# The value product of latent attention in two passes over paired high and low weights, with a later hand-over of each pair's result

## The chip, the cores and the metric

One core of a Trainium2 chip runs the whole kernel. The metric is the device time of one execution in microseconds (us); smaller is better. The matrix engine is PE (its weight loads are listed as PEld), the vector engine DVE, the scalar engine ACT, GpSimd POOL, and SP issues the transfers. Each engine executes its own list of instructions in order and waits on semaphores for the others.

## The reference, cut to what matters

Two layers of a decoder trunk over 512 tokens of width 1024: a layer with latent attention, a layer with an mLSTM mixer, each followed by a squared-ReLU MLP. The change is inside the attention of the first layer: 16 heads, query and key width 96, value width 64, in blocks of 128 queries that see the keys up to their own block.

```
for blk in range(S // ATTN_BLOCK):                       # 4 blocks of 128 queries
    s = (q_n . k_n + q_r . k_r) * scale                  # 128 x k_end per head
    p = softmax(where(k_idx <= q_idx, s, -inf))
    outs.append(einsum('bhqk,bhkd->bqhd', p, v[:, :k_end]))
o = concatenate(outs, axis=1).reshape(B, S, 16 * 64)
return o @ w_o
```

## The kernel before

Every float32 factor x is split into x_hi, a copy rounded to the matrix engine's fp32r format, and x_lo = x - x_hi, also in fp32r. A product of two such factors is three matmuls: hi by lo, hi by hi, lo by hi. ACT mostly makes the high parts (a cast), DVE or POOL the low ones (a subtraction).

Attention runs over 16 heads in 8 pairs. Every engine has a function `attention(head)`, and the order of its calls is written out by hand; it is that order that decides who waits behind whom. A head passes through these steps:

- `q_half(head + 2, ...)` on PE: the query product of the head after next, 12 matmuls of 512 columns in two halves. `q_table` (DVE) scales it into `qtmp`, `q_high` (ACT) and `q_low` (DVE) split it. In odd heads `k_high` (ACT, two casts of 64x512) and `k_low` (DVE, two subtractions of 64x512) split the keys of the next pair, which `k_product` (PE, even heads) made.
- `turn_p(head, b)` on PE for b = 0..3: transposes the (b + 1) probability blocks of query block b into PSUM. `pt_high` (ACT) and `pt_low` (DVE) split them into `pth` and `ptl`. `turn_p(head, b)` may not start before `pt_low` has emptied the bank two steps back (`t_lo`).
- `scores(head + 1, b)` on PE: the scores of the next head, in a ring of three PSUM banks. `row_max` (DVE) and `exp` (ACT) empty them. `scores(head + 1, 3)` reuses the bank of b = 0, so it waits for `exp(head + 1, 0)` (semaphore `s_exp`).
- `weigh(head)` on PE: the value product. A 128x128 weight tile holds the values of 128 keys. The tensors `vh` and `vl` have three column groups of 64: the pair's even head, zeros, the odd head. The window of 128 columns that starts at 64 * e covers the head's values and the zeros, so both heads of a pair accumulate into one PSUM bank, `B_PV`, rows 0 to 63 and 64 to 127. It makes three passes of four matmuls (512, 384, 256 and 128 columns): `vh` by `pth`, `vl` by `pth`, `vh` by `ptl`.
- After the second head of a pair, `turn_scales` and `spread_scales` (PE), `row_scales` (DVE), `rows_turned` and `rows_spread` (ACT) bring the reciprocal row sums into `r_b`. At the start of the next even head `o_scaled` (DVE) multiplies bank `B_PV` by `r_b` into `o_norm(i)`, `o_high` (ACT) rounds it into `uh` and `o_low` (POOL) makes `ul`. `weigh` of the next even head waits for `o_scaled` (semaphore `o_new`).
- `strip_low` on POOL makes the low parts of the weight strip that a head three steps ahead needs (`split` on ACT makes the high ones).

`attention_end` replaces the last two heads on PE: with no further queries to make, it puts parts of the output projection (`out_products(k)`, six matmuls of 512 columns each, which need `uh` and `ul` of pair k, semaphore `o_lo`) between the steps, and `out_products(5..7)` after the last `weigh`.

Of the kernel before, what the change touches and what calls it, by code (L numbers as in the profile page):

```python
# [5 lines left out]
F32 = mybir.dt.float32  # L6
F32R = mybir.dt.float32r
I32 = mybir.dt.int32
ALU = mybir.AluOpType
# [5 lines left out]
P = 128  # L15
# [87 lines left out]
def trunk(nc, a, out):  # L103
    ctx = ExitStack()
    with ctx:
# [5 lines left out]
        def sem(name):  # L111
            return ctx.enter_context(nc.semaphore(name))
# [69 lines left out]
        cql = A("cql", [P, 4, S], F32R)  # L182
        ckvh = A("ckvh", [P, 2, S], F32R)
        ckvl = A("ckvl", [P, 2, S], F32R)
        vh = A("vh", [P, TT, 3 * VD], F32R)
        vl = A("vl", [P, TT, 3 * VD], F32R)
        prob = A("prob", [P, P * TT * (TT + 1) // 2])
        cos = A("cos", [P, S])
        sin = A("sin", [P, S])
# [24 lines left out]
        def v_slot(i):  # L214

            return v_all[:, i, :].rearrange("p (t e n) -> p t e n", t=TT, e=2)

        def heads_of(t):

            return t[:, :, :].rearrange("p t (r n) -> p t r n", r=3)[:, :, 0::2, :]  # L220

        def gap_of(t):

            return t[:, :, VD:2 * VD]

        def prob_of(b):

# [3 lines left out]
        def o_norm(i):  # L231

            return diag[:, i % 2, :]
# [57 lines left out]
        def bank(b):  # L291
            return ps[:, b, :]
# [49 lines left out]
        v_hi, v_lo = sem("v_hi"), sem("v_lo")  # L342
        s_mm, s_max, s_exp = sem("s_mm"), sem("s_max"), sem("s_exp")
        t_mm, t_hi, t_lo = sem("t_mm"), sem("t_hi"), sem("t_lo")
        w_mm, o_new, o_hi, o_lo = sem("w_mm"), sem("o_new"), sem("o_hi"), sem("o_lo")
        r_inv, rt_mm, rt_ready, r_mm, r_ready, pick_ready = (sem("r_inv"), sem("rt_mm"), sem("rt_ready"), sem("r_mm"),
                                                             sem("r_ready"), sem("pick_ready"))
# [224 lines left out]
        def _(pool):  # L572
# [15 lines left out]
            g.tensor_copy(onesr[:], ones[:, 0:2])  # L588
            g.tensor_copy(identr[:], ident[:])
            g.tensor_copy(maskr[:], mask_s[:]).then_inc(consts, 1)  # L590
            for t in (vh, vl):
                g.memset(gap_of(t).bitcast(F32), 0.0)

            def norm_adds(norm, end=False):

# [12 lines left out]
            def strip_low(n, kind, p=0):  # L608

                pool.wait_ge(whi_ready, p * 2 + (n + 1))  # L610
                for src, hi, lo in split_parts(kind, n % 2):
                    last = g.tensor_tensor(lo, src, hi.bitcast(F32), ALU.subtract)
                last.then_inc(wlo_ready, 1)
# [17 lines left out]
            def v_low(i):  # L631

                pool.wait_ge(v_hi, i + 1)
                g.tensor_tensor(heads_of(vl), v_slot(i), heads_of(vh).bitcast(F32), ALU.subtract).then_inc(v_lo, 1)

            def o_low(i):

                pool.wait_ge(o_hi, i + 1)
                g.tensor_tensor(ul[:, i, :], o_norm(i), uh[:, i, :].bitcast(F32), ALU.subtract).then_inc(o_lo, 1)
# [4 lines left out]
            for head in range(HEADS):  # L644
                if head % 2 == 0:
                    v_low(head // 2)
                    if head:
                        o_low(head // 2 - 1)
                if head + 3 < HEADS:
                    strip_low(N_PAIR + head + 3, "kq" if head % 2 else "q")  # L650
                elif head + 3 < HEADS + 2:
                    strip_low(N_WO + head + 3 - HEADS, "full")

            def low_hidden(layer, q, lead, per):
                for j in range(8):
# [76 lines left out]
        def _(act):  # L732
# [116 lines left out]
            def exp(head, b):  # L849

                z = 4 * head + b
                act.wait_ge(s_max, z + 1)
                if head:
                    act.wait_ge(t_mm, z - 3)
                sc.activation(prob_of(b), ps[:, B_S + z % S_RING, 0:P * (b + 1)], ACT.Exp,
                              bias=nmax[:, b:b + 1],
                              accum_out=rsum[:, 4 * (head % 2) + b:4 * (head % 2) + b + 1]).then_inc(s_exp, 1)

            def pt_high(head, b):

                z = 4 * head + b
                if b == 0 and head >= 2:
                    act.wait_ge(w_mm, head - 1)
                act.wait_ge(t_mm, z + 1)
                sc.copy(pth[head % 2][:, 0:b + 1, P * b:P * b + P],
                        ps[:, B_PT + z % 2, 0:P * (b + 1)].rearrange("p (j q) -> p j q", q=P)).then_inc(t_hi, 1)

            def v_high(i):

                if i:  # L870
                    act.wait_ge(w_mm, 2 * i)
                sc.copy(heads_of(vh), v_slot(i)).then_inc(v_hi, 1)

            def o_high(i):

                act.wait_ge(o_new, i + 1)
                sc.copy(uh[:, i, :], o_norm(i)).then_inc(o_hi, 1)
# [37 lines left out]
            def attention(head):  # L915

                i, second = head // 2, head % 2
                nxt = head + 1 < HEADS
                if not second:
                    v_high(i)  # L920
                    if i:
                        o_high(i - 1)
                elif nxt:
                    for e in range(2):
                        k_high(e, i + 1)
                pt_high(head, 0)
                pt_high(head, 1)
                if head + 3 < HEADS:
                    split(N_PAIR + head + 3, "q" if not second else "kq")
                elif head + 3 == HEADS:  # L930
                    split(N_WO)
                if second:
                    rows_turned(i)
                pt_high(head, 2)
                if nxt:
                    exp(head + 1, 0)
                pt_high(head, 3)
                if nxt:
                    exp(head + 1, 1)
                if head + 2 < HEADS:  # L940
                    q_high(head + 2)
                if nxt:
                    exp(head + 1, 2)
                    exp(head + 1, 3)
                if second:
                    rows_spread(i)
                if head + 2 == HEADS:
                    split(N_WO + 1)

            for head in range(HEADS):  # L950
                attention(head)
            o_high(PAIRS - 1)

            def residual_stage(n0, t0, norm, gain):
# [188 lines left out]
        def _(dve):  # L1143
# [176 lines left out]
            def row_scales(i):  # L1320
# [5 lines left out]
                own.link(v.tensor_copy(rinv2[:, 0:8], rinv[:]))  # L1326
                low(rinv2[:, 8:16], rinv[:], rinv2[:, 0:8]).then_inc(r_inv, 1)

            def o_scaled(i):

                dve.wait_ge(w_mm, 2 * i + 2)
                dve.wait_ge(r_ready, i + 1)
                if i >= 2:
                    dve.wait_ge(o_lo, i - 1)
                v.tensor_tensor(o_norm(i), bank(B_PV), r_b[:], ALU.mult).then_inc(o_new, 1)

            for e in range(2):
                k_low(e, 0)
# [6 lines left out]
            def attention(head):  # L1345

                nxt = head + 1 < HEADS
                i, second = head // 2, head % 2
                if second:
                    row_scales(i)  # L1350
                elif i:
                    o_scaled(i - 1)
                if second and nxt:
                    for e in range(2):
                        k_low(e, i + 1)
                pt_low(head, 0)
                pt_low(head, 1)
                if head + 2 < HEADS:
                    q_table(head + 2)
                if nxt:  # L1360
                    row_max(head + 1, 0)
                pt_low(head, 2)
                if nxt:
                    row_max(head + 1, 1)
                    row_max(head + 1, 2)
                pt_low(head, 3)
                if nxt:
                    row_max(head + 1, 3)
                if head + 2 < HEADS:
                    q_low(head + 2)  # L1370

            for head in range(HEADS):
                attention(head)
            o_scaled(PAIRS - 1)
            dve.wait_ge(o_lo, PAIRS - 1)
            dve.wait_ge(o_hi, PAIRS)
# [244 lines left out]
        def _(pe):  # L1621
# [177 lines left out]
            def weigh(head):  # L1799

                e = head % 2
                cols = slice(VD * e, VD * e + P)
                pe.wait_ge(t_hi, 4 * head + 4)
                pe.wait_ge(v_hi, head // 2 + 1)
                if e == 0 and head:
                    pe.wait_ge(o_new, head // 2)
                for j in range(TT):
                    mm(ps[:, B_PV, P * j:S], vh[:, j, cols], pth[e][:, j, P * j:S], start=(e + j == 0), stop=False)
                pe.wait_ge(v_lo, head // 2 + 1)
                for j in range(TT):  # L1810
                    mm(ps[:, B_PV, P * j:S], vl[:, j, cols], pth[e][:, j, P * j:S], start=False, stop=False)
                pe.wait_ge(t_lo, 4 * head + 4)
                for j in range(TT):
                    last = mm(ps[:, B_PV, P * j:S], vh[:, j, cols], ptl[e][:, j, P * j:S], start=False,
                              stop=(e == 1 and j == TT - 1))
                last.then_inc(w_mm, 1)

            def turn_scales(i):
# [376 lines left out]
```

## Time and profile before

| | |
|---|---|
| Median of 3 runs | 1213.28 us (1212.80 to 1213.59) |
| The profiled execution's own time | 1213.74 us |
| Span of its trace | 1211.8 us |
| PE busy | 1201.4 us, 99% of the span |
| DVE, ACT, POOL busy | 602.2, 455.1, 278.9 us |
| Attention, from about 79 us to 225 us of the span | PE, DVE, ACT and POOL all work |

How to read the trace's rows: the time at which a row starts, its duration, the engine, the source line, what is written and read, and how many instructions are merged in the row. A square bracket gives the time that the engine sat idle before the row and what ended it. Starts of matmuls overlap the ends of the ones before: the distance between two starts is what a matmul costs PE, and the duration shown is its latency. A busy PE may therefore still hide waits shorter than that latency.

### The profile page before, as it was taken

What the parts mean: (1) busy time and instruction counts of PE and PEld (TensorE: products, weight loads), DVE (VectorE), ACT (ScalarE), POOL (GpSimd) and SP (SyncE); (2) the same over time, 40 slices, a digit from 0 to 9 for tenths busy, and PEclk for the clock granted to TensorE, in tenths of its full rate; (3) what the DMA queues carried; (4) which work ended last, traced back from release to release, by engine and by line L of the source; (5) the groups of instructions that cost most, each with busy time, mean ns of one, the idle gap of its engine ahead of it and who ended that gap; (6) DMA issues with size and microseconds to landing.
All of it is one profiled execution on the core that took longest, in us unless ns stands there. A gap on an engine that the chain in (4) does not pass through costs nothing.

```text
span 1211.8 us, 15769 instructions
## 1 busy us (share of the span) xinstructions
PE 1201.4 (99%) x6130; PEld 1016.2 (84%) x6130; DVE 602.2 (50%) x818; ACT 455.1 (38%) x734; POOL 278.9 (23%) x286
## 2 busy tenths in 40 slices
PE   9999999999999999999999999999999999999998
PEld 8878888888888888888879899988888888888887
DVE  6766666455334334344357645657443443433432
ACT  5567777433212222123344255644321221222234
POOL 2324234242002002012212145633210110210212
PEclk9999999999999999999999999999999999999999
DMA  6111113232333323322233534513233233332221
GB/s 202 40 35 29 34 26 105 71 104 70 105 104 102 99 78 104 104 93 81 77 100 104 148 92 98 114 38 99 75 105 104 74 102 103 104 104 82 93 74 70
DMA packets 117513, 107.42 MB, mean 89 GB/s; under 512 B 21350, under 2 KB 115780, under 8 KB 117452
## 3 DMA queue, kind: packets, MB, share of 16 engines
q1 hardware_dynamic: 117420, 106.56, 29.2%
q8 instruction: 43, 0.70, 0.3%
q14 instruction: 18, 0.15, 0.0%
q10 hardware_dynamic: 32, 0.01, 0.0%
HBM read 104.45 MB, written 2.11 MB: 88 GB/s over the span
## 4 chain that ended last, share of the span: by engine, by line
PE 82%; DVE 1%; issue 0%; ACT 0%; POOLq 0%; POOL 0%; DVEq 0%; ACTq 0%
PE ps L1630 25%; PE ps L1632 25%; PE ps L1631 25%; PE ps L2072 1%; PE ps L2074 1%; PE ps L2073 1%; PE ps L2101 1%; PE ps L2103 0%; PE ps L2102 0%; PE ps L1924 0%; PE ps L1926 0%; PE ps L1925 0%; PE ps L2084 0%; PE ps L1994 0%; PE ps L1656 0%
## 5 line engine op out<-in xcount | busy, mean ns | idle before, releaser
L747 ACT CAST whi<-raw 128x2048 fp32r<-128x2048 f32 (+4 forms) x148 | 183.0, 1266 | 262.1 <-PE ps L1632 254.7
L1151 DVE TENSOR_TENSOR wlo<-raw,whi 128x2048 fp32r<-128x2048 f32 (+3 forms) x90 | 197.6, 2198 | 151.9 <-ACT whi L747 151.8
L1630 PE MATMUL ps<-xl,whi 128*128 128x512 f32 (+1 forms) x624 | 245.1, 393 | 0.1
L1631 PE MATMUL ps<-xh,whi 128*128 128x512 f32 (+1 forms) x624 | 242.9, 389 | 0.0
L1632 PE MATMUL ps<-xh,wlo 128*128 128x512 f32 (+1 forms) x624 | 242.9, 389 | 0.0
L1630 PE MATMUL ps<-ul,whi 128*128 128x512 f32 x576 | 224.7, 390 | 0.3 <-DVE wlo L1151 0.3
L1632 PE MATMUL ps<-uh,wlo 128*128 128x512 f32 x576 | 224.2, 389 | 0.0
L1631 PE MATMUL ps<-uh,whi 128*128 128x512 f32 x576 | 224.1, 389 | 0.0
L657 POOL TENSOR_TENSOR ul<-sq,uh 128x512 fp32r<-128x512 f32 x64 | 83.7, 1308 | 521.1 <-ACT uh L1000 521.1
L1382 DVE TENSOR_TENSOR h<-ps,h 128x512 f32<-128x512 f32 x78 | 53.6, 689 | 181.5 <-PE ps L1632 178.0
L1000 ACT CAST uh<-sq 128x512 fp32r<-128x512 f32 x64 | 39.7, 620 | 266.3 <-DVE sq L1414 266.3
L1630 PEld LDWEIGHTS ps<-xl,whi 128*128 128x128 f32 (+1 forms) x624 | 116.6, 187 | 26.4 <-issue 1.9
L1631 PEld LDWEIGHTS ps<-xh,whi 128*128 128x128 f32 (+1 forms) x624 | 116.6, 187 | 25.5 <-issue 1.0
L1632 PEld LDWEIGHTS ps<-xh,wlo 128*128 128x128 f32 (+1 forms) x624 | 116.6, 187 | 25.1
L1630 PEld LDWEIGHTS ps<-ul,whi 128*128 128x128 f32 x576 | 108.1, 188 | 22.9 <-DVE wlo L1151 0.7
L1632 PEld LDWEIGHTS ps<-uh,wlo 128*128 128x128 f32 x576 | 108.1, 188 | 22.6
L1631 PEld LDWEIGHTS ps<-uh,whi 128*128 128x128 f32 x576 | 108.1, 188 | 22.3
L1408 DVE TENSOR_TENSOR diag<-ps,r_a 128x512 f32<-128x512 f32 x64 | 44.0, 688 | 105.6 <-PE ps L1632 105.6
L602 POOL TENSOR_TENSOR acc<-acc,sq 128x512 f32<-128x512 f32 x30 | 48.7, 1623 | 128.2 <-ACT sq L761 127.6
L1630 PE MATMUL ps<-wlo,xh 128*128 128x256 f32 x256 | 73.5, 287 | 0.0
L1631 PE MATMUL ps<-whi,xh 128*128 128x256 f32 x256 | 72.4, 283 | 0.0
L1632 PE MATMUL ps<-whi,xl 128*128 128x256 f32 x256 | 72.4, 283 | 0.0
(276 smaller groups left out, 1689.3 us busy)
## 6 DMA issues: line engine op xcount, KB each, us to landing
raw<-in_mlp_w SPq DMA_DIRECT2D x64, 1024.0 KB, 5.2
raw<-in_mlstm_w_in SPq DMA_DIRECT2D x12, 1024.0 KB, 5.3
raw<-in_mla_w_o SPq DMA_DIRECT2D x4, 1024.0 KB, 4.9
raw<-in_mlstm_w_o SPq DMA_DIRECT2D x4, 1024.0 KB, 5.2
raw<-in_mla_w_uq SPq DMA_DIRECT2D x16, 192.0 KB, 2.5
x_tok<-in_x SPq DMA_DIRECT2D x4, 512.0 KB, 6.9
raw<-in_mla_w_in SPq DMA_DIRECT2D x2, 1024.0 KB, 5.7
mx<-m_rows SPq DMA_DIRECT2D x8, 256.0 KB, 3.8
```

The lines of the kernel that those rows point to most:

```text
L602: g.tensor_tensor(acc[:], acc[:], sq[:, k % 2, :], ALU.add).then_inc(acc_add, 1)
L657: g.tensor_tensor(ul[:, j, :], sq[:, j % 2, :], uh[:, j, :].bitcast(F32), ALU.subtract) \
L747: last = sc.copy(hi, src)
L1000: sc.copy(uh[:, m, :], sq[:, m % 2, :]).then_inc(u_hi, 1)
L1151: last = v.tensor_tensor(lo, src, hi.bitcast(F32), ALU.subtract)
L1382: return v.tensor_tensor(h[:, m, :], bank(t % RING), h[:, m, :], ALU.add)
L1408: v.tensor_tensor(diag[:, m % 2, :], bank((t0 + m) % RING), r_a[:], ALU.mult) \
L1630: mm(o, ah, bl, start=first, stop=False)
L1631: mm(o, ah, bh, start=False, stop=False)
L1632: ins = mm(o, al, bh, start=False, stop=last)
L2072: mm(o[:, 0:VW], hi, mvh[:, e, j, :], start=(j == 0), stop=False)
L2073: mm(o[:, 0:P], hi, mvl[:, e, j, :], start=False, stop=False)
```

## The change

The columns of high and low values stand side by side in one tensor `vhl` of four groups of 64: even head high, even head low, odd head low, odd head high. `weigh` uses the 128 columns of the head as weights, so one pass over `pth` gives both the high and the low value product, in the two halves of the bank's rows; a second pass over `ptl` completes it. Each head now fills the whole bank, so it is emptied head by head: `o_second` (ACT) moves the half that belongs to the low columns into `o_part` in SBUF, at the rows of the other half, and `o_add` (DVE) adds the two into `o_norm(i)`. `weigh(head)` waits for `o_add` of the head before (`o_sum`). `o_scaled` now multiplies `o_norm(i)` by `r_b` in SBUF, and stands, as do `o_high` and `o_low`, at the end of the next even head and no longer at its start; on POOL `strip_low` comes ahead of `o_low`.

```diff
-        vh = A("vh", [P, TT, 3 * VD], F32R)
-        vl = A("vl", [P, TT, 3 * VD], F32R)
+        vhl = A("vhl", [P, TT, 4 * VD], F32R)
+        o_part = A("o_part", [P, S])
...
+        def v_parts(low):
+
+            quarters = vhl[:, :, :].rearrange("p t (r n) -> p t r n", r=4)
+            return quarters[:, :, 1:3, :] if low else quarters[:, :, 0::3, :]
...
-            for t in (vh, vl):
-                g.memset(gap_of(t).bitcast(F32), 0.0)
...
                 if head % 2 == 0:
                     v_low(head // 2)
-                    if head:
-                        o_low(head // 2 - 1)
                 if head + 3 < HEADS:
                     strip_low(N_PAIR + head + 3, "kq" if head % 2 else "q")
                 elif head + 3 < HEADS + 2:
                     strip_low(N_WO + head + 3 - HEADS, "full")
+                if head % 2 == 0 and head:
+                    o_low(head // 2 - 1)
...
+            def o_second(head):
+
+                e = head % 2
+                act.wait_ge(w_mm, head + 1)
+                if head >= 2:
+                    act.wait_ge(o_sum, head - 1)
+                sc.copy(o_part[64 * e:64 * e + 64, :], ps[64 - 64 * e:128 - 64 * e, B_PV, :]).then_inc(o_moved, 1)
...
                     v_high(i)
-                    if i:
-                        o_high(i - 1)
...
                 pt_high(head, 1)
+                if head:
+                    o_second(head - 1)
...
                     exp(head + 1, 3)
+                if i and not second:
+                    o_high(i - 1)
...
+            o_second(HEADS - 1)
             o_high(PAIRS - 1)
...
+            def o_add(head):
+
+                i, rows = head // 2, slice(64 * (head % 2), 64 * (head % 2) + 64)
+                dve.wait_ge(o_moved, head + 1)
+                if head % 2 == 0 and i >= 2:
+                    dve.wait_ge(o_lo, i - 1)
+                v.tensor_tensor(o_norm(i)[rows, :], ps[rows, B_PV, :], o_part[rows, :], ALU.add).then_inc(o_sum, 1)
+
             def o_scaled(i):
 
-                dve.wait_ge(w_mm, 2 * i + 2)
+                dve.wait_ge(o_sum, 2 * i + 2)
                 dve.wait_ge(r_ready, i + 1)
-                if i >= 2:
-                    dve.wait_ge(o_lo, i - 1)
-                v.tensor_tensor(o_norm(i), bank(B_PV), r_b[:], ALU.mult).then_inc(o_new, 1)
+                v.tensor_tensor(o_norm(i), o_norm(i), r_b[:], ALU.mult).then_inc(o_new, 1)
...
                 if second:
                     row_scales(i)
-                elif i:
-                    o_scaled(i - 1)
...
                     q_table(head + 2)
+                if head:
+                    o_add(head - 1)
                 if nxt:
                     row_max(head + 1, 0)
...
                     q_low(head + 2)
+                if i and not second:
+                    o_scaled(i - 1)
...
+            o_add(HEADS - 1)
             o_scaled(PAIRS - 1)
...
-                cols = slice(VD * e, VD * e + P)
+                cols = slice(P * e, P * e + P)
                 pe.wait_ge(t_hi, 4 * head + 4)
-                pe.wait_ge(v_hi, head // 2 + 1)
-                if e == 0 and head:
-                    pe.wait_ge(o_new, head // 2)
+                pe.wait_ge(v_lo, head // 2 + 1)
+                if head:
+                    pe.wait_ge(o_sum, head)
                 for j in range(TT):
-                    mm(ps[:, B_PV, P * j:S], vh[:, j, cols], pth[e][:, j, P * j:S], start=(e + j == 0), stop=False)
-                pe.wait_ge(v_lo, head // 2 + 1)
-                for j in range(TT):
-                    mm(ps[:, B_PV, P * j:S], vl[:, j, cols], pth[e][:, j, P * j:S], start=False, stop=False)
+                    mm(ps[:, B_PV, P * j:S], vhl[:, j, cols], pth[e][:, j, P * j:S], start=(j == 0), stop=False)
                 pe.wait_ge(t_lo, 4 * head + 4)
                 for j in range(TT):
-                    last = mm(ps[:, B_PV, P * j:S], vh[:, j, cols], ptl[e][:, j, P * j:S], start=False,
-                              stop=(e == 1 and j == TT - 1))
+                    last = mm(ps[:, B_PV, P * j:S], vhl[:, j, cols], ptl[e][:, j, P * j:S], start=False,
+                              stop=(j == TT - 1))
```

## Rows read from the trace of the kernel before

**Rows 1.** The page: busy time of the engines, and granted clock in 40 slices.

```profile
PE 1201.4 (99%) x6130; PEld 1016.2 (84%) x6130; DVE 602.2 (50%) x818; ACT 455.1 (38%) x734; POOL 278.9 (23%) x286
...
PEclk9999999999999999999999999999999999999999
```

**Rows 2.** Attention in one stretch: us, then busy us and instructions by engine.

```profile
86.00:224.00 138.00, 137.06 (x824) 119.67 (x823) 87.97 (x188) 98.46 (x275) 49.79 (x58) 1.00 0.16 45
```

**Rows 3.** Timeline, end of an even head and start of the odd one.

```profile
141.29 0.76 PE L1808 MATMUL ps<-xh,vh 128*128 128x512 f32 x4
141.62 0.19 ACT L855 ACTIVATION_READ_ACCUMULATOR prob<-ps,nmax 128x1 f32 x1
141.71 1.18 ACT L842 CAST xh<-ps 64x512 fp32r<-64x512 f32 x2
...
141.88 0.80 PE L1811 MATMUL ps<-xh,vl 128*128 128x512 f32 x4
...
142.37 1.40 DVE L1156 TENSOR_TENSOR xl<-ps,xh 64x512 fp32r<-64x512 f32 x2
...
142.52 0.80 PE L1814 MATMUL ps<-xl,vh 128*128 128x512 f32 x4
...
143.16 0.44 PE L1766 MATMUL ps<-cql,whi 128*128 128x512 f32 x1
```

**Rows 4.** Timeline, the middle of that odd head.

```profile
144.97 0.54 ACT L865 CAST pt_b<-ps 128x128 fp32r<-128x128 f32 x2 [2.08 <-PE ps L1796]
...
145.40 1.11 ACT L747 CAST whi<-raw 128x256 fp32r<-128x256 f32 x4
...
146.53 0.69 DVE L1301 TENSOR_TENSOR qtmp<-ps,tab 128x512 f32<-128x512 f32 x1 [0.56 <-PE ps L1768]
...
146.97 0.48 ACT L865 CAST pt_b<-ps 128x384 fp32r<-128x384 f32 x1
...
147.36 0.29 DVE L1310 TENSOR_REDUCE nmax<-ps 128x1 f32<-128x128 f32 x1
...
147.69 0.37 ACT L855 ACTIVATE prob<-ps,nmax 128x128 f32<-128x128 f32 x1 [0.24 <-DVE nmax L1310]
147.96 0.20 ACT L855 ACTIVATION_READ_ACCUMULATOR prob<-ps,nmax 128x1 f32 x1
...
148.67 0.44 PE L1783 MATMUL ps<-xl,xh 128*128 128x512 f32 x1
```

**Rows 5.** Timeline, the same place of the even head before it.

```profile
137.02 0.69 DVE L1301 TENSOR_TENSOR qtmp<-ps,tab 128x512 f32<-128x512 f32 x1 [0.56 <-PE ps L1768]
...
138.34 0.19 ACT L855 ACTIVATION_READ_ACCUMULATOR prob<-ps,nmax 128x1 f32 x1
...
139.05 0.44 PE L1783 MATMUL ps<-xl,xh 128*128 128x512 f32 x1
...
140.32 0.68 DVE L1310 TENSOR_REDUCE nmax<-ps 128x1 f32<-128x512 f32 x1
...
140.91 0.68 DVE L1156 TENSOR_TENSOR xl<-qtmp,xh 128x512 fp32r<-128x512 f32 x1
```

**Rows 6.** Timelines by engine, the last three heads.

```profile
202.79 4.60 POOL L612 TENSOR_TENSOR wlo<-raw,whi 128x2048 fp32r<-128x2048 f32 x1 [8.77 <-ACT whi L747]
...
205.94 2.00 DVE L1156 TENSOR_TENSOR xl<-qtmp,xh 128x512 fp32r<-128x512 f32 x1
...
209.82 0.52 PE L1796 MATMUL ps<-ident,prob 128*128 128x128 f32 x3 [0.94 <-DVE xl L1156]
...
215.24 1.89 ACT L747 CAST whi<-raw 128x2048 fp32r<-128x2048 f32 x1
```

**Rows 7.** Timelines by engine, from the last value product on.

```profile
224.10 0.80 PE L1814 MATMUL ps<-pt_b,vh 128*128 128x512 f32 x4
...
224.94 0.69 DVE L1335 TENSOR_TENSOR diag<-ps,r_b 128x512 f32<-128x512 f32 x1 [2.75 <-PE ps L1814]
...
226.39 0.69 DVE L1156 TENSOR_TENSOR ul<-diag,uh 128x512 fp32r<-128x512 f32 x1 [0.76 <-ACT uh L877]
...
227.56 0.39 PE L1924 MATMUL ps<-ul,whi 128*128 128x512 f32 x1
```

More of the change, by code:

```diff
@@ L216, in v_slot @@
             return v_all[:, i, :].rearrange("p (t e n) -> p t e n", t=TT, e=2)
[L218 to L224, printed above, removed]
+        def v_parts(low):
+            quarters = vhl[:, :, :].rearrange("p t (r n) -> p t r n", r=4)
+            return quarters[:, :, 1:3, :] if low else quarters[:, :, 0::3, :]
         def prob_of(b):
@@ L344, in trunk @@
         t_mm, t_hi, t_lo = sem("t_mm"), sem("t_hi"), sem("t_lo")
+        o_moved, o_sum = sem("o_moved"), sem("o_sum")
         w_mm, o_new, o_hi, o_lo = sem("w_mm"), sem("o_new"), sem("o_hi"), sem("o_lo")
@@ L633, in v_low @@
                 pool.wait_ge(v_hi, i + 1)
-                g.tensor_tensor(heads_of(vl), v_slot(i), heads_of(vh).bitcast(F32), ALU.subtract).then_inc(v_lo, 1)
+                g.tensor_tensor(v_parts(True), v_slot(i), v_parts(False).bitcast(F32), ALU.subtract).then_inc(v_lo, 1)
             def o_low(i):
@@ L871, in v_high @@
                     act.wait_ge(w_mm, 2 * i)
-                sc.copy(heads_of(vh), v_slot(i)).then_inc(v_hi, 1)
+                sc.copy(v_parts(False), v_slot(i)).then_inc(v_hi, 1)
+            def o_second(head):
[4 more added lines that the diff above has]
+                sc.copy(o_part[64 * e:64 * e + 64, :], ps[64 - 64 * e:128 - 64 * e, B_PV, :]).then_inc(o_moved, 1)
             def o_high(i):
```

## The prediction, made before the changed kernel ran

> **What bounds the kernel now.** I read the page first. PE is busy 99% of the span and its granted clock is in the top tenth in all 40 slices [rows 1], so it runs at the 2.4 GHz level throughout and a matmul taken away is worth its full place in the queue, unless another engine then becomes late. The change touches only attention, so the second view is that stretch: of 138 us PE is busy 137.06, ACT 98.46, DVE 87.97, POOL 49.79 [rows 2]. PE bounds the stage, but ACT already works 71% of it. Since PE's busy time can hide waits shorter than a matmul's latency, the third view is the timeline of single heads, where the reader should look at the distances of starts, and at how close each wait that PE passes is to being late. Those margins decide this case.
>
> **The pass that goes.** Three passes of `weigh` start at 141.29, 141.88 and 142.52, and the next matmul after them at 143.16 [rows 3]: 0.59, 0.64 and 0.64 us. The first pass of a head now does the work of two, so one of the 0.64 us goes, in each of 16 heads: 16 x 0.64 = 10.2 us. If instead the short pass were the one saved, it would be 16 x 0.59 = 9.4 us; I take 0.64, since a second pass of the same shapes, followed by the same matmul, stays. The trace has no row for `vhl` as weights, but the tile is 128x128 from consecutive columns as before, and I leave its load and its stream as they are.
>
> The Trainium skill, "TensorE: Matmul & The Clock Gate", section "Back-to-back issue gap", gives an isolated warm matmul N/2.4 + 2.5 ns. For the 1280 columns of a pass that is an estimate of 543 ns, so the sum would be 8.7 us instead of 10.2. The row's 0.64 us is for the real sequence with its weight loads, and it decides.
>
> **What is added to ACT and DVE.** `o_second` reads 64x512 from PSUM; the nearest row is `k_high`, two in 1.18 us, 0.59 each [rows 3]. `o_add` reads 64x512 from PSUM and writes SBUF; the nearest is `k_low`, two in 1.40, 0.70 each [rows 3]. Over the 138 us with 15 heads that is 8.9 us more for ACT (98.5 to 107.3) and 10.5 for DVE (88.0 to 98.5), against about 129 us of PE: neither becomes the bound by total. What matters is where they stand.
>
> `o_second` stands behind `pt_high(head, 1)`, ahead of `split`. In the odd head ACT runs `pt_high` at 144.97, `split` at 145.40, and `pt_high(head, 2)` at 146.97 [rows 4]. With the copy, `split` starts near 145.9 and ends near 147.0, and `pt_high(head, 2)` comes near 147.3, so ACT is free for `exp` near 147.7, where it was used at 147.69. That still fits.
>
> `o_add` stands between `q_table` and `row_max(head + 1, 0)`. DVE starts instructions of 0.68 us about 0.60 apart (140.32, 140.91) [rows 5]. In the odd head `q_table` starts at 146.53, so `o_add` comes at 147.13 and `row_max` at 147.73 instead of 147.36. From `row_max` to `exp` was 0.33 us (147.36, 147.69), and the accumulator read ends 0.47 us behind that (147.96 + 0.20) [rows 4]: now 148.53. `scores(head + 1, 3)` waits for it and starts at 148.67: 0.14 us left of 0.51. In the even head the same steps from 137.02 give 138.22, 138.55 and 139.02 against a start of 139.05 [rows 5]: nothing left of a margin of 0.52. The matmul's weight load starts some 0.06 us before it and a semaphore must travel, so I put 0.06 us of stall on each of 14 heads, 0.8 us. Bounds: zero, if DVE starts `row_max` sooner; and 0.2 us a head, 2.8 in all, if `o_add` holds DVE its whole 0.70 us and the signal takes 0.1 more.
>
> **What is moved.** `o_scaled`, `o_high` and `o_low` go from the start of an even head to its end. At the start this removes nothing from PE in steady state, for it has no wait there. At the end it puts `o_scaled` behind `q_low` (140.91, so about 141.55 to 142.25), and `o_high` behind that on ACT (to about 142.9). Queued behind `o_high` are `k_high` (was 141.71) and then `pt_high` of the odd head; behind `k_high` are `k_low` and PE's `turn_scales`. `k_high` now ends near 144.05. PE's odd head starts 0.64 earlier, so the probabilities are ready for `pt_high` at 144.97 - 0.64 = 144.33. ACT had idled 2.08 us there [rows 4]; some 0.3 are left. `k_low` ends near 144.75, before PE wants it. Free, but if the chain slips more than 0.3 us, odd heads pay.
>
> `v_high` and `v_low` cast as many elements as before. The wait for `v_lo` at the start of `weigh` is met several us earlier. On POOL, `o_low` behind `strip_low` matters only where a strip is long: the last, full one takes 4.60 us [rows 6] and starts when ACT's cast of 1.89 us is over (about 217) [rows 6], so the result of pair 6 is ready near 223, ahead of the last `weigh`. Nothing. The two memsets of the zeros go, at the start of POOL's list, which nobody waits for.
>
> **The last heads.** In head 14 PE waits 0.94 us before `turn_p(14, 2)`, behind `pt_low` [rows 6]. `o_high` no longer stands ahead of `pt_high(14, 0)`, so part of it comes back; but `q_low` is held until POOL's strip ends (2.00 us instead of 0.68) [rows 6], and the new copy moves that strip 0.5 us later, so I expect 0.3 us. In head 15 `o_high(6)`, 0.62 us, stands ahead of the 1.89 us cast and so ahead of `pt_high(15, 0)`, while PE arrives 1.6 us sooner: about 0.4 us of wait. Net: -0.1 us, bounds -0.9 to +0.9.
>
> The Trainium skill, "SBUF — State Buffer", section "Who interferes with whom", says that a DVE instruction with two SBUF inputs contends with a GpSimd instruction that reads SBUF, and the 2.00 us row agrees. `o_scaled` becomes such an instruction. If it met a strip it would wait; by the trace POOL's strip of an even head is over by then, so the sum is unchanged.
>
> Behind the last `weigh`, PE has `out_products(5)` and `(6)` before it needs pair 7. The passes end at 224.90 and `ul` is ready at 226.39 + 0.69 = 227.08; PE starts `out_products(7)` at 227.56 without a wait [rows 7]. Now `o_second` (0.59) and `o_add` (0.70) come in front, so with handing over 3.5 us pass instead of 2.2, and PE's cover is 227.56 - 224.90 = 2.66. I take 0.9 us of new wait (bounds 0.7 and 1.3).
>
> **The sum.** -10.2 + 0.8 + 0.1 + 0.9 = -8.4 us. The profiled execution took 1213.74 us around a span of 1211.8, so it should become 1205.3; the median of the runs, 1213.28, stands 0.46 lower: 1204.9. What follows attention is bound by PE too and its strips are requested by released buffers, so it moves along whole.
>
> **The rivals.** *The softmax chain takes the gain.* PE's wait for `exp(head + 1, 0)` is real and larger, 0.2 to 0.6 us a head: 3 to 8 us of the 10.2 go, time 1206.5 to 1212. For it: both margins of half a microsecond are used up by my own count, and `o_add` is unseen. Against: DVE overlaps starts. *All of it arrives*: no stall, head 14's 0.94 us returned, the tail at 0.7: -10.2 - 0.9 + 0.7 = -10.4, time 1202.9. Against: the zero margin of even heads. *The change does not do what it says*: PE, freed, waits for the chain by exactly the pass removed, 1213. Against: ACT and DVE have over 20 us of idle time left. *Slower*: the hand-over at a pair's end. DVE's `o_scaled` behind `q_low`, then `o_high`, then `k_high`, then `pt_high` in a row delay the odd head. It decides from about 1.05 us of real PE wait in each of 8 odd heads, that is 0.3 us of idle plus some 0.8 us through `pt_low` to `turn_p`, a slip of 2.1 us; at 3 us of slip it is 8 x 1.9 = 15 us against 8.4, time 1220. For it: three engines in series on a thin 0.3 us. Against: each link has a row, and they add up to no such slip.
>
> **How the numbers follow.** Forecast as reckoned, stalls of 0 to 0.2 us a head (1203.3 to 1206.5): 0.62. Softmax chain: 0.20. All of it: 0.09. No change: 0.04. Slower: 0.05. The likeliest is 1204.9. Its own bounds are those of the terms; down to 1202.9 the range takes in the case in which all arrives, and up to 1209.0 most of the softmax case; that leaves out under 2 in 10. 0.2%, 2.4 us, is about what a measurement here can tell from no change. All of the first and third cases and nearly all of the softmax case are faster by more: 0.90; within it 0.05, slower 0.05.
>
> **What would show it.** Two starts of `weigh` passes 0.6 us apart and no third; `scores(head + 1, 3)` starting at most 0.1 us behind its old place after `scores(head + 1, 2)`; `row_max` about 0.4 us later than before; ACT idle about 0.3 us and not 2 before `pt_high` of odd heads; a PE wait of 0.9 us before `out_products(7)`; every stage behind attention of the same length. Wrong would be: waits of PE in the middle of heads over 0.2 us, `k_high` later than 143.5 on this time scale, or weight loads of `vhl` longer than 0.19 us.

## The result, and the profile after

The changed kernel takes 1206.28 us (median of 5 runs, 1205.84 to 1206.52) against 1213.28 us: 7.0 us less, a ratio of 0.9942 with a 95% interval of 0.9931 to 0.9953. The forecast was 1204.9 with a range of 1202.9 to 1209.0. The profiled execution took 1205.84 us around a span of 1204.1.

First the page and the windows of the changed kernel, the lines that answer to [rows 1, 2].

```profile
PE 1192.3 (99%) x6066; PEld 1006.1 (84%) x6066; DVE 611.0 (51%) x834; ACT 462.2 (38%) x750; POOL 278.5 (23%) x284
...
PEclk9999999999999999999999999999999999999999
...
86.00:224.00 138.00, 135.66 (x790) 115.75 (x789) 99.31 (x206) 107.86 (x292) 50.16 (x58) 1.00 0.18 51
```

64 matmuls are gone (6130 to 6066), the clock is unchanged, and ACT and DVE now work 108 and 99 us of that stretch. (The stretch is the same in time, not in work: attention ends some 8 us earlier in this trace, so its last part now holds the stage behind.)

Next the timeline of the changed kernel, end of an even head and start of the odd one, answering to [rows 3].

```profile
137.38 0.74 PE L1824 MATMUL ps<-xh,vhl 128*128 128x512 f32 x4
137.96 0.80 PE L1827 MATMUL ps<-xl,vhl 128*128 128x512 f32 x4
...
138.60 0.44 PE L1782 MATMUL ps<-cql,whi 128*128 128x512 f32 x1
...
138.34 0.62 ACT L881 CAST uh<-diag 128x512 fp32r<-128x512 f32 x1 [0.42 <-DVE diag L1348]
138.87 1.18 ACT L838 CAST xh<-ps 64x512 fp32r<-64x512 f32 x2
140.41 0.54 ACT L861 CAST pt_b<-ps 128x128 fp32r<-128x128 f32 x2 [0.35 <-PE ps L1812]
```

Two passes, 0.58 and 0.64 us, and the third is gone. `o_high` (L881) stands ahead of `k_high` (L838), and ACT idles 0.35 us and no longer 2.08 before `pt_high`: still early enough.

The middle of the odd head and of the even head of the changed kernel, answering to [rows 4, 5]:

```profile
141.97 0.69 DVE L1308 TENSOR_TENSOR qtmp<-ps,tab 128x512 f32<-128x512 f32 x1 [0.43 <-PE ps L1784]
142.58 0.67 DVE L1342 TENSOR_TENSOR diag<-ps,o_part 64x512 f32<-64x512 f32 x1
143.17 0.27 DVE L1317 TENSOR_REDUCE nmax<-ps 128x1 f32<-128x128 f32 x1
...
143.44 0.42 PE L1799 MATMUL ps<-xl,xh 128*128 128x384 f32 x1
...
144.10 0.44 PE L1799 MATMUL ps<-xl,xh 128*128 128x512 f32 x1
...
132.79 0.69 DVE L1308 TENSOR_TENSOR qtmp<-ps,tab 128x512 f32<-128x512 f32 x1 [0.56 <-PE ps L1784]
133.51 0.69 DVE L1342 TENSOR_TENSOR diag<-ps,o_part 64x512 f32<-64x512 f32 x1
134.24 0.29 DVE L1317 TENSOR_REDUCE nmax<-ps 128x1 f32<-128x128 f32 x1
...
134.83 0.19 ACT L851 ACTIVATION_READ_ACCUMULATOR prob<-ps,nmax 128x1 f32 x1
...
134.15 0.42 PE L1799 MATMUL ps<-xl,xh 128*128 128x384 f32 x1
...
135.07 0.19 PEld L1799 LDWEIGHTS ps<-xl,xh 128*128 128x128 f32 x1 [0.30 <-ACT prob L851]
135.07 0.50 PE L1799 MATMUL ps<-xl,xh 128*128 128x512 f32 x1
135.41 0.40 PE L1800 MATMUL ps<-xh 128*128 128x512 f32 x1
```

In the odd head DVE starts `q_table`, `o_add` and `row_max` 0.61 and 0.59 us apart, and PE starts `scores(head + 1, 3)` 0.66 us behind `scores(head + 1, 2)`, without a wait. In the even head the distances are 0.72 and 0.73. The accumulator read of `exp(head + 1, 0)` ends at 135.02, and PE starts 0.92 us behind `scores(head + 1, 2)`: 0.26 us of wait. The matmul behind it comes 0.34 us later and not 0.27, so each such wait costs 0.33 us. No idle time is printed at PE's own rows, since the latency of the matmul before covers it; the distance of starts shows it, and so does the row of the weight load (PEld), which names `exp`'s row as what ended 0.30 us of waiting. The same numbers stand in six even heads (2 to 12).

Head 13 waits at the same step, but for another reason. ACT there casts a full strip. The rows of ACT and PE:

```profile
193.47 0.58 ACT L876 COPY o_part<-ps 64x512 f32<-64x512 f32 x1
193.96 1.90 ACT L743 CAST whi<-raw 128x2048 fp32r<-128x2048 f32 x1
...
196.04 0.46 ACT L861 CAST pt_b<-ps 128x384 fp32r<-128x384 f32 x1
196.42 0.35 ACT L851 ACTIVATE prob<-ps,nmax 128x128 f32<-128x128 f32 x1
...
196.92 0.50 PE L1799 MATMUL ps<-xl,xh 128*128 128x512 f32 x1 [0.15 <-ACT prob L851]
```

This is an odd head, so its add is at rows 0 to 63, and `row_max` is done at 195.94, before ACT comes to `exp`. The last link is ACT: the copy `o_second` stands ahead of the cast, and against PE's `scores(14, 2)` the cast starts 0.62 us later than in the kernel before (1.98 us ahead of it in place of 2.60). PE starts `scores(14, 3)` 0.98 us behind `scores(14, 2)` and the next matmul 0.34 behind that: 0.4 us lost. That it is not the add is shown by the experiments below with the add moved or at other rows, where this distance stays 0.97 to 0.98 us; that it is the copy is argued from these rows, no run took the copy away.

The last heads, answering to [rows 6, 7]: timelines by engine of the changed kernel.

```profile
199.01 2.06 DVE L1163 TENSOR_TENSOR xl<-qtmp,xh 128x512 fp32r<-128x512 f32 x1
...
201.12 0.33 PE L1803 MATMUL ps<-xh,xl 128*128 128x128 f32 x1 [0.63 <-DVE xl L1163]
...
210.33 0.52 PE L1812 MATMUL ps<-ident,prob 128*128 128x128 f32 x3 [0.22 <-DVE pt_b L1163]
...
216.12 0.58 ACT L876 COPY o_part<-ps 64x512 f32<-64x512 f32 x1 [0.79 <-PE ps L1827]
...
216.73 0.69 DVE L1342 TENSOR_TENSOR diag<-ps,o_part 64x512 f32<-64x512 f32 x1 [2.71 <-ACT o_part L876]
217.46 0.69 DVE L1348 TENSOR_TENSOR diag<-diag,r_b 128x512 f32<-128x512 f32 x1
...
218.52 0.39 PE L1939 MATMUL ps<-uh,wlo 128*128 128x512 f32 x1
219.66 0.50 PE L1937 MATMUL ps<-ul,whi 128*128 128x512 f32 x1 [0.75 <-DVE ul L1163]
```

Behind the last value product the copy (L876), the add (L1342) and the scaling (L1348) follow one another, and PE starts `out_products(7)` 1.14 us behind the matmul before it, where 0.23 is usual: 0.91 us lost. In head 15 `turn_p(15, 2)` (210.33) starts 0.4 us late: `pt_high(15, 0)` now stands behind `o_high` and the cast of a full strip on ACT, as the prediction had it. In head 14 the hold of `q_low` by GpSimd's strip (2.06 us in place of 0.68) makes PE wait 0.63 us, in `scores(15, 0)` at 201.12; before, the same hold cost 0.94 us at `turn_p(14, 2)`.

**Where the time came from.** The two traces must be compared from a mark inside attention. The first value product of the kernel before, and of the changed one:

```profile
85.89 0.57 PE L1808 MATMUL ps<-xh,vh 128*128 128x512 f32 x2
```

```profile
84.88 0.69 PE L1824 MATMUL ps<-xh,vhl 128*128 128x512 f32 x3
```

That 1.0 us arises in the first 7 us, in the warm-up matmuls (the first 20 take 4.64 us in one trace and 4.00 in the other), and is not the change's: a kernel with the old layout (the experiment with the late hand-over alone) has its mark at 84.92, and one with the new layout (GpSimd's strips in quarters) at 85.87. From the mark to `out_products(7)` it is 141.67 us before (227.56 - 85.89) and 134.78 after (219.66 - 84.88): 6.9 us less, which agrees with the 7.0 of the medians. By rows: 16 x 0.64 = 10.2 us removed; 6 x 0.33 = 2.0 lost in even heads, 0.4 in head 13, 0.4 before `turn_p(15, 2)`, 0.9 before `out_products(7)`; 0.2 returned in head 14. Net 6.7, and 0.2 stays unassigned. Behind `out_products(7)`'s first matmul the next starts 0.33 us later in place of 0.23, another 0.1 lost; from the mark to the end of the span it is 1125.9 against 1119.2, 6.7 us less.

### The profile page after: what moved, and what is told of

It is laid out like the page before. It is cut to its first block, busy times and chain, and to the rows that moved or that the text cites. A ratio compares the mean times of both kernels' runs of the same rounds, so it can differ in the third digit from the quotient of the medians.

```text
span 1204.1 us, 15691 instructions
## 1 busy us (share of the span) xinstructions
PE 1192.3 (99%) x6066; PEld 1006.1 (84%) x6066; DVE 611.0 (51%) x834; ACT 462.2 (38%) x750; POOL 278.5 (23%) x284
## 4 chain that ended last, share of the span: by engine, by line
PE 94%; DVE 3%; ACT 2%; issue 1%; POOL 0%; POOLq 0%; DVEq 0%; ACTq 0%
PE ps L1646 27%; PE ps L1648 26%; PE ps L1647 26%; PE ps L1782 1%; PE ps L1784 1%; PE ps L1783 1%; PE ps L1812 1%; PE ps L2085 1%; PE ps L1824 1%; PE ps L2087 1%; PE ps L1827 1%; PE ps L2086 1%; PE ps L1799 1%; PE ps L1803 1%; PE ps L1800 1%
```

## Experiments

All changes are against the changed kernel unless said otherwise. Times are medians. The kernel before ran on the same chip beside each of three groups. It took 1212.95 us beside the add at rows 0 to 63, the late add, the single pass and GpSimd's order; 1213.44 beside the late hand-over alone, the pass made twice, the filled wait and the quarters; 1213.13 beside the add at rows 64 to 127 and the single pass with the late add. The changed kernel itself did not run again in these groups, so a difference to its 1206.28 is good to about 0.5 us. Smaller effects are read from the distances in the traces.

**The add at rows 0 to 63 for both heads**

```diff
-                sc.copy(o_part[64 * e:64 * e + 64, :], ps[64 - 64 * e:128 - 64 * e, B_PV, :]).then_inc(o_moved, 1)
+                sc.copy(o_part[0:64, :], ps[64:128, B_PV, :]).then_inc(o_moved, 1)
...
-                i, rows = head // 2, slice(64 * (head % 2), 64 * (head % 2) + 64)
+                i, rows = head // 2, slice(0, 64)
```

> The two halves of both heads are added at rows 0 to 63 (input, second input and output), so the odd heads' results are in the wrong rows; all instructions, shapes and waits are as in the changed kernel. Theory (DVE holds an instruction whose operands start at another partition than the one before, here rows 64 against 0, and then the next one too): in even heads the distances from q_table to o_add and from o_add to row_max fall from 0.72 and 0.73 us to 0.60 each, and PE's 0.26 us of wait before scores(head + 1, 3) in the 6 even heads goes: 1.6 us faster, 1204.7. Rival (the wait comes from the length of the add, or from GpSimd's strip beginning at that moment): the distances stay 0.72, 1206.3.

1204.85 us, 1.4 less than the changed kernel. DVE in the even head of this run:

```profile
132.41 0.69 DVE L1308 TENSOR_TENSOR qtmp<-ps,tab 128x512 f32<-128x512 f32 x1 [0.56 <-PE ps L1784]
133.02 0.67 DVE L1342 TENSOR_TENSOR diag<-ps,o_part 64x512 f32<-64x512 f32 x1
133.62 0.27 DVE L1317 TENSOR_REDUCE nmax<-ps 128x1 f32<-128x128 f32 x1
```

The distances are now 0.61 and 0.60. Engine, shapes, waits and neighbours are the same; only the rows differ. PE starts `scores(head + 1, 3)` 0.67 us behind `scores(head + 1, 2)` again, but the next matmul still comes 0.33 to 0.34 us later in place of 0.28: 0.06 us a head are left in the six even heads.

**Its mirror: the add at rows 64 to 127 for both heads**

```diff
-                sc.copy(o_part[64 * e:64 * e + 64, :], ps[64 - 64 * e:128 - 64 * e, B_PV, :]).then_inc(o_moved, 1)
+                sc.copy(o_part[64:128, :], ps[0:64, B_PV, :]).then_inc(o_moved, 1)
...
-                i, rows = head // 2, slice(64 * (head % 2), 64 * (head % 2) + 64)
+                i, rows = head // 2, slice(64, 128)
```

> The mirror of the run at rows 0 to 63: both heads of a pair are added at rows 64 to 127, so the even heads' results are in the wrong rows. Theory (start partition against the instructions around it): now the odd heads too show 0.72 us from q_table to o_add and 0.73 to row_max, exp comes 0.25 us later there, and PE waits about 0.15 to 0.25 us before scores(head + 1, 3) in 7 odd heads as well: 1.0 to 1.7 us slower than the changed kernel, 1207.3 to 1208. Rival (something else of the even heads makes them slow): 1206.3 and odd distances of 0.6.

1207.91 us, 1.6 more than the changed kernel. DVE in the odd head of this run:

```profile
143.07 0.69 DVE L1308 TENSOR_TENSOR qtmp<-ps,tab 128x512 f32<-128x512 f32 x1 [0.44 <-PE ps L1784]
143.80 0.69 DVE L1342 TENSOR_TENSOR diag<-ps,o_part 64x512 f32<-64x512 f32 x1
144.52 0.29 DVE L1317 TENSOR_REDUCE nmax<-ps 128x1 f32<-128x128 f32 x1
```

0.73 and 0.72 us, now in the odd head, and PE loses 0.21 us in each of six odd heads (1 to 11). Both directions agree: an instruction on DVE that starts at row 64 between two that start at row 0 waits until the one before is done, and the next one waits too, together 0.25 us. The Trainium skill, "VectorE: DVE Perf Modes", section "Two Vector instructions with no wait between them", gives a model by which an instruction is held until all earlier DVE instructions have finished, when an input or the output starts in another group of 32 partitions than in the last instruction that read or wrote the same memory. The two runs agree.

The trace of the kernel before had a sign of this: the two subtractions of `k_low`, which read PSUM from row 0 and then from row 64, take 1.40 us [rows 3], 0.04 more than two whole instructions of 0.68 one behind the other; with starts 0.60 apart they would take 1.28, and ACT's second cast, which the second one needs, was done at 142.89, before such a start. The prediction used that row for the add's length, not for the distance to its neighbours.

**The add behind `row_max`**

```diff
-                if head:
-                    o_add(head - 1)
                 if nxt:
                     row_max(head + 1, 0)
+                if head:
+                    o_add(head - 1)
```

> o_add stands behind row_max(head + 1, 0) in place of ahead of it. Theory (PE's only repeated wait is for exp(head + 1, 0), which that add delays): the wait in 6 even heads goes, 1.6 us faster, 1204.7; the tail is unchanged. Rival (DVE's queue as a whole is late, so the wait moves to another step such as scores(head + 1, 2) or weigh): within 0.5 us of 1206.3.

1204.24 us, 2.0 less; ratio to the kernel before 0.9927 (0.9914 to 0.9941). PE in the even head:

```profile
133.72 0.42 PE L1799 MATMUL ps<-xl,xh 128*128 128x384 f32 x1
...
134.38 0.44 PE L1799 MATMUL ps<-xl,xh 128*128 128x512 f32 x1
```

0.66 us: the wait is gone, and it did not move to another step. The held add is still there (133.40 to 134.13 on DVE, 0.73), but nobody waits for what follows it. The wait of the even heads had two parents, then: the add's place, and its start at row 64. With the place mended nothing of it is left; with the rows mended, 0.06 of 0.33 us a head.

**One pass of the value product**, the low parts of the probabilities left out of it, its wait kept:

```diff
                 for j in range(TT):
-                    mm(ps[:, B_PV, P * j:S], vhl[:, j, cols], pth[e][:, j, P * j:S], start=(j == 0), stop=False)
-                pe.wait_ge(t_lo, 4 * head + 4)
-                for j in range(TT):
-                    last = mm(ps[:, B_PV, P * j:S], vhl[:, j, cols], ptl[e][:, j, P * j:S], start=False,
-                              stop=(j == TT - 1))
+                    if j == TT - 1:
+                        pe.wait_ge(t_lo, 4 * head + 4)
+                    last = mm(ps[:, B_PV, P * j:S], vhl[:, j, cols], pth[e][:, j, P * j:S], start=(j == 0),
+                              stop=(j == TT - 1))
```

> The second pass of weigh (the low parts of the probabilities by the values) is left out, its wait kept. Theory (a pass of four matmuls is worth 0.64 us in each of 16 heads as long as PE bounds): 10 us faster than the changed kernel, 1196; at most 1.5 us of it lost to waits. Rival (the softmax chain on DVE and ACT is about to take over): waits of 0.3 us or more appear in each head, and under 6 us are gained, 1200 or more.

1198.49 us: 7.8 us less than the changed kernel, between the two expectations and nearer the theory's. A further pass removed does not come through whole. I guessed that the missing 2.4 us were again the wait for `exp(head + 1, 0)`, and tried the single pass with the late add:

> The late add and one pass of weigh together (the low parts of the probabilities are left out of the value product). The single pass with the early add gained 7.8 us of 10.2. Theory (what was lost there was again the wait for exp(head + 1, 0)): with the late add 9.5 to 10.2 us come off 1204.2, 1194 to 1194.7. Rival (DVE and ACT cannot deliver a head in 7.6 us, so the wait appears at other steps): 1196 or more.

1198.54 us: only 5.7 us less than the late add with two passes, and the guess falls. The waits that weight loads met in this run:

```profile
PEld ps L1835 <- issue: 2.7, 6, 0.5
...
PEld ps L1812 <- issue: 2.4, 7, 1.0
PEld ps L1843 <- issue: 1.7, 8, 0.4
PEld ps L1803 <- DVE xl L1163: 1.4, 1, 1.4
```

L1835 (`turn_scales`, which waits for `k_lo`) is new, and L1812 (`turn_p`, which waits for `pt_low`) now waits in odd heads too, where with two passes it waited once, in head 15. Both stand behind `o_high`, `k_high`, `k_low`: the serial hand-over at a pair's end, with the 0.35 us of idle time it had left. From one `weigh` to the next, an odd head took 8.21 us with the late add and takes 8.03: 0.46 of the 0.64 us are lost, in five heads. That is 2.3 of the 4.5 us that did not arrive. Another 1.8 is lost in heads 13 to 15, whose lengths hardly move (8.60, 8.41 and 7.76 us before, 8.57, 8.38 and 7.72 now): there PE waits for `exp(14, 0)` behind the full strip's cast, for `q_low` behind GpSimd's strip (1.4 us) and for `pt_low` of head 15 (1.0). So the hand-over is the next limit in the middle heads, and the last three have limits of their own already.

**GpSimd's order undone**

```diff
                     v_low(head // 2)
+                    if head:
+                        o_low(head // 2 - 1)
                 if head + 3 < HEADS:
                     strip_low(N_PAIR + head + 3, "kq" if head % 2 else "q")
...
-                if head % 2 == 0 and head:
-                    o_low(head // 2 - 1)
```

> Only the order on GpSimd is undone: o_low ahead of strip_low, while o_scaled and o_high stay at the end of the even head. Theory (strip_low then waits for o_high, and its strip is what PE's odd head begins with): o_low ends near 140.3 on the changed kernel's time scale and the strip near 141.9, where PE wants it at 138.6, so 3.3 us of PE wait at the start of the odd heads, 6 times: 20 us slower, about 1226. Rival (the strip has slack enough): 1206.3.

1236.16 us, 29.9 more than the changed kernel; I had expected 20. PE at the start of an odd head, and two windows (columns as in [rows 2], the granted clock third from the end):

```profile
154.05 0.79 PE L1782 MATMUL ps<-cql,whi 128*128 128x512 f32 x1 [3.09 <-POOL wlo L608]
```

```profile
124.00:144.00 20.00, 16.90 (x81) 14.00 (x80) 10.28 (x23) 11.88 (x35) 6.30 (x9) 0.83 0.12 27
144.00:154.00 10.00, 6.87 (x42) 5.79 (x40) 7.67 (x16) 6.78 (x18) 2.77 (x4) 0.98 0.01 2
```

The wait is the one expected: 3.1 us, six times, 18.6 in all. The rest is the clock. In the changed kernel it is 1.00 throughout; here, with 3 us of waiting in each pair, it is 0.83 of full speed over 20 us, so it spent part of the stretch at its lower level of 1.2 GHz. The sizes fit: over the profiled execution's span of 1236.7 us the mean granted clock is 0.989, which is 13.6 us of full speed missing, and this span is 32.6 us longer than the changed kernel's, 14.0 more than the waits. So GpSimd's new order is no ornament: with the hand-over at the end of an even head, it is what keeps the strip ready.

**The old kernel with the late hand-over alone**: in the kernel before, only `o_scaled`, `o_high` and `o_low` moved to where the change has them.

```diff
-                    if head:
-                        o_low(head // 2 - 1)
...
+                if head % 2 == 0 and head:
+                    o_low(head // 2 - 1)
...
-                    if i:
-                        o_high(i - 1)
...
                     exp(head + 1, 3)
+                if i and not second:
+                    o_high(i - 1)
...
-                elif i:
-                    o_scaled(i - 1)
...
                     q_low(head + 2)
+                if i and not second:
+                    o_scaled(i - 1)
```

> The kernel before (three passes, one bank for a pair), with only o_scaled, o_high and o_low moved to where the change has them. Theory (the bank must be emptied ahead of weigh of the even head, and o_scaled now ends behind q_low, near 142.25 where weigh began at 141.29): about 1 us of PE wait in each of 7 even heads, 7 to 8 us slower, 1221. Rival (the move is free, as in the changed kernel): 1213.

1219.36 us against 1213.44, 5.9 slower. The value product of an even head in this run:

```profile
143.62 0.83 PE L1808 MATMUL ps<-xh,vh 128*128 128x512 f32 x4 [0.89 <-DVE diag L1335]
```

0.9 us of wait in each of six heads (2 to 12), and 0.3 in head 14. The late hand-over needs the bank emptied head by head, which `o_second` and `o_add` do.

**The first pass made twice**, so that PE has its old number of matmuls:

```diff
+                for j in range(TT):
+                    mm(ps[:, B_PV, P * j:S], vhl[:, j, cols], pth[e][:, j, P * j:S], start=False, stop=False)
                 pe.wait_ge(t_lo, 4 * head + 4)
```

> The changed kernel with its first pass made twice, so that PE has the old number of matmuls (the high part of the probabilities is counted twice). Theory (a pass is 0.64 us in each head and the waits that the change added stay): 10.2 us slower than the changed kernel, 1216.5, so 3.2 us above the kernel before. Rival (part of the pass hides in the new waits): 1213 to 1214.

1215.77 us, 9.5 more than the changed kernel and 2.3 more than the kernel before (ratio 1.0021, 1.0011 to 1.0030). So the other parts of the change cost 2.3 us where PE has its old work. The 9.5 is 0.7 short of 16 x 0.64; in this run PE comes later and the waits of heads 14 and 15 are mostly covered, as the rival had it for all of them: head 14 is no longer than with two passes (8.41 us against 8.40), head 15 only 0.22 us longer.

**Filling the wait at the end**: on top of the late add, PE makes half a tile of the next strip before it asks for the last pair.

```diff
...
-                out_products(range(5, KD))
+                out_products(range(5, KD - 1))
+                next_strip(range(0, 4))
+                out_products(range(KD - 1, KD))
+                next_strip(range(4, KD))
...
```

> o_add behind row_max as in the run before, and behind out_products(6) PE makes half a tile of the next strip (12 matmuls, 2.8 us) before it waits for the last pair. Theory (0.75 us of wait before out_products(7) is lost time and nothing behind it is late): 0.8 us faster than with the late add alone, 1203.4. Rival (the first residual tiles and the cast of the strip after next come 2.8 us later and give it back): 1204.2 or more.

1203.79 us beside 1213.44: 9.65 us less than the kernel before beside it, where the late add alone had 8.71 less. PE around the place:

```profile
219.50 0.39 PE L1957 MATMUL ps<-uh,wlo 128*128 128x512 f32 x1
219.72 0.39 PE L1940 MATMUL ps<-ul,whi 128*128 128x512 f32 x1
```

`out_products(7)` (L1940) follows at the usual 0.22 us. The wait is gone. The size of the gain, 0.9 us, is a difference of two groups and no more certain than they are; by the two medians alone it is 0.45. From the first value product to the end of the span, the trace of the late add alone has 1117.35 us and this one 1116.24, 1.1 less.

**GpSimd's full strips in quarters**, on top of that:

```diff
...
-                for src, hi, lo in split_parts(kind, n % 2):
+                parts = split_parts(kind, n % 2)
+                if kind == "full" and n >= N_WO:
+                    parts = [tuple(t[:, 512 * c:512 * c + 512] for t in parts[0]) for c in range(4)]
+                for src, hi, lo in parts:
...
```

> As the run with the half tile, and GpSimd makes the low parts of the two full strips of attention in four instructions of 512 columns in place of one of 2048. Theory (q_low of the last head is held until GpSimd's instruction ends, 2.06 us instead of 0.68, which costs PE 0.63 us in head 14): q_low waits for one quarter at most, 0.6 us faster, 1202.8. Rival (it is held until the whole strip is done, or the four instructions come so much later that others wait): 1203.4 or more.

1203.66 us, not to be told from 1203.79. The rows of DVE, GpSimd and PE:

```profile
198.17 1.24 DVE L1166 TENSOR_TENSOR xl<-qtmp,xh 128x512 fp32r<-128x512 f32 x1
...
195.10 5.45 POOL L611 TENSOR_TENSOR wlo<-raw,whi 128x512 fp32r<-128x512 f32 x4 [2.80 <-ACT whi L746]
...
200.70 0.52 PE L1815 MATMUL ps<-ident,prob 128*128 128x128 f32 x3 [0.33 <-DVE xl L1166]
```

`q_low` is held 0.56 us and no longer 1.38, as the theory says, but GpSimd's work grew from 4.6 to 5.4 us, and PE now waits 0.33 us one step further on, for `pt_low`. The hold is real, but shortening it is worth little here: head 14 is 0.24 us shorter in the trace (8.18 against 8.42), which the medians cannot tell.

## Why the prediction was right, and where it was off

The direction, the mechanism and the range were right; the point was 1.4 us too low. That the range held owes something to luck, as the stall shows.

**The pass** came off as reckoned: 0.64 us from start to start, in all 16 heads.

**The stall at `scores(head + 1, 3)`** is the term that was mis-sized. I named the place, the chain (`q_table`, `o_add`, `row_max`, `exp`) and its margin, and put 0.06 us on each of 14 heads, 0.8 in all. It measured 0.33 in each of six even heads, 0.4 in head 13 and zero in the other heads: 2.4 us. For the six even heads, 2.0 us, the step that failed was "DVE starts instructions of 0.68 us about 0.60 apart", read from instructions that all start at row 0 and carried over to one that starts at row 64. With the add at rows 0 to 63 those heads lose 0.06 us each, just what I had put. For head 13, 0.4 us, another step failed: I checked the copy ahead of `split` with a cast of 1.11 us and not with the full strip's 1.90. My upper bound of 0.2 us a head was too low for the even heads; it held in sum, 2.8, because the odd heads up to 11 lost nothing. That is luck.

Two of my own signs came out against me. A wait of PE in the middle of a head over 0.2 us was to show that I was wrong, and six heads have 0.26; `row_max` was to come about 0.4 us later, and it does in odd heads (0.37), but comes 0.73 later in even ones.

**The addition to ACT and DVE** was right: 0.58 and 0.69 us each, neither the bound.

**The moved hand-over** was right to 0.1 us: `k_high` starts 0.27 us behind PE's odd head (reckoned 0.4), 0.35 us of idle time is left (reckoned 0.3), no wait. That it is the next limit in the middle heads, the single pass with the late add showed.

**The last heads**: reckoned 0.3 returned and 0.4 lost, measured 0.2 and 0.4. (The recorded text calls the net -0.1; the sum rightly uses +0.1.) **The wait at the end**: reckoned 0.9, measured 0.91 plus 0.1 for the slower start after it.

**The rivals.** The waits for `exp(head + 1, 0)` took 2.4 us; the rival wanted 3 to 8 in all and did not come. But it wanted 0.2 to 0.6 us a head, and six heads lie in that. The line between it and the forecast was also drawn badly: the forecast's own terms, with stalls of 0 to 0.2 us a head, give 1204.1 to 1206.9 and not 1203.3 to 1206.5; 1206.28 lies in both. "Slower" by the hand-over did not come. That the change does nothing is refuted by the 7.0 us.

## What to carry to other kernels

When matmuls are taken from a tensor engine that is busy all the time, the gain is their start-to-start distance less what the added links do to the narrowest margin; list the margins of all its waits first, and put added work behind the instruction with the narrowest one, not ahead of it. Price an added vector instruction with its start partition: one that starts elsewhere than its neighbours costs itself and the next their overlap. Where a result is handed over later, every queue it passes needs its order looked at again, since one subtraction ahead of a strip was worth 30 us here.

## What was not expected of the hardware

- The 0.25 us that one DVE instruction at row 64 costs between instructions at row 0 (0.72 and 0.73 us apart in place of 0.61 and 0.59).
- After a wait of 0.26 us, PE's next start comes 0.34 us later in place of 0.27, so a short wait costs 0.07 us more than its length. With the add at rows 0 to 63, where the wait itself has shrunk to 0.01 us or less, the next start is still 0.33 to 0.34 us away.
- The first value product lies at 85.89 us in one trace and at 84.92 in another of the same layout: two single traces can differ by 1.0 us before the first value product.
- Six waits of 3.1 us cost 18.6 us themselves, and the kernel 29.9, with a granted clock of 0.83 where it had been 1.00.
